# Old states' part of the sampled outputs: C as stationary operand in column strips instead of the state

## What is computed

```python
# G=4 groups, E=8 heads each, P=64 values per head, N=128 state entries
y_diag = jnp.einsum('bcgls,bcgels,bcsgep->bclgep', CB, Lmat, xd)
states = jnp.einsum('bcsgn,bcges,bcsgep->bcgepn', Bm, decay_states, xd)
states = jnp.concatenate([h0.reshape(nb, G, E, P, N)[:, None], states], axis=1)
new_states = jnp.einsum('bgezc,bcgepn->bzgepn', decay_chunk, states)
states_in, final = new_states[:, :-1], new_states[:, -1]
y_off = jnp.einsum('bclgn,bcgepn,bcgel->bclgep', Cm, states_in, jnp.exp(A_cs))
y = (y_diag + y_off).reshape(nb, L, SSD_HEADS, P)
```

## Time and profile before

| | us |
|---|---|
| median of 3 runs | 1894.99 (1893.29 to 1895.34) |
| the profiled execution | 1895.05 |
| its span in the profile | 1892.9 |
| PE busy | 1862.7 (98%) |
| DVE busy | 1111.5 (59%) |
| ACT busy | 647.4 (34%) |
| POOL busy | 137.7 (7%) |

### The profile page before, as it was taken

How to read it: one execution, slowest core, us unless ns; L and a number is a source line. 1 busy time by engine, 2 the same in 40 slices (tenths; PEclk the granted TensorE clock), 3 DMA queues, 4 the chain that set the end, 5 groups by cost and what they waited for, 6 DMA issues and landing times.

```text
span 1892.9 us, 31449 instructions
## 1 busy us (share of the span) xinstructions
PE 1862.7 (98%) x12735; PEld 1817.8 (96%) x12735; DVE 1111.5 (59%) x1368; ACT 647.4 (34%) x842; POOL 137.7 (7%) x257
## 2 busy tenths in 40 slices
PE   8999999999999999999999999999999999999998
PEld 7999999999999999999989989998999999999998
DVE  6443443345777866767777877885855433442444
ACT  5221332123577742334244235233332211221223
POOL 3000000000012121111111101100200000000000
PEclk9999999999999999999999999999999999999999
DMA  5222222222422253354354335335622222222222
GB/s 147 73 71 78 73 72 78 78 67 66 133 69 79 62 160 99 115 153 112 90 151 125 101 95 164 107 106 189 208 70 78 70 74 78 77 67 78 78 64 81
DMA packets 273342, 186.14 MB, mean 98 GB/s; under 512 B 7452, under 2 KB 260580, under 8 KB 273008
## 3 DMA queue, kind: packets, MB, share of 16 engines
q1 hardware_dynamic: 239840, 129.52, 23.8%
q0 software_dynamic: 10624, 36.91, 6.4%
q10 hardware_dynamic: 22800, 18.62, 3.0%
HBM read 162.48 MB, written 22.53 MB: 98 GB/s over the span
## 4 chain that ended last, share of the span: by engine, by line
PE 88%; DVE 6%; ACT 3%; issue 2%; DMA 0%; ACTq 0%; DVEq 0%
PE pu L647 80%; PE pn L899 1%; PE pn L849 1%; DVE w_lo L1403 1%; PE pn L867 1%; PE pn L744 1%; PE pn L871 1%; PE pn L890 1%; PE pu L706 0%; DVE bc L1397 0%; DVE squares L1397 0%; PE pn L838 0%; PE pu L909 0%; PE pn L664 0%; DVE xc L1397 0%
## 5 line engine op out<-in xcount | busy, mean ns | idle before, releaser
L1403 DVE TENSOR_TENSOR w_lo<-w_raw,w_hi 128x1024 fp32r<-128x1024 f32 x240 | 296.5, 1235 | 460.2 <-ACT w_hi L985 458.7
L647 PE MATMUL pu<-act_hi,w_hi 128*128 128x320 f32 x1952 | 456.9, 315 | 6.7 <-DVE xc L1397 2.2
L647 PE MATMUL pu<-act_lo,w_hi 128*128 128x320 f32 x1952 | 447.2, 310 | 1.1 <-DVE act_lo L1446 1.0
L647 PE MATMUL pu<-act_hi,w_lo 128*128 128x320 f32 x1952 | 446.7, 310 | 0.0
L985 ACT ACTIVATE w_hi<-w_raw 128x1024 fp32r<-128x1024 f32 x240 | 253.5, 1056 | 520.8 <-PE pu L647 519.6
L647 PEld LDWEIGHTS pu<-act_hi,w_hi 128*128 128x128 f32 x1952 | 327.3, 189 | 21.3 <-issue 17.1
L647 PEld LDWEIGHTS pu<-act_lo,w_hi 128*128 128x128 f32 x1952 | 328.5, 189 | 2.4 <-DVE act_lo L1446 1.5
L647 PE MATMUL pu<-x_hi,w_hi 128*128 128x320 f32 x1440 | 329.3, 310 | 1.3 <-DVE ff_g L1459 1.3
L647 PEld LDWEIGHTS pu<-act_hi,w_lo 128*128 128x128 f32 x1952 | 328.7, 189 | 0.0
L647 PE MATMUL pu<-x_lo,w_hi 128*128 128x320 f32 x1440 | 328.5, 309 | 0.0
L647 PE MATMUL pu<-x_hi,w_lo 128*128 128x320 f32 x1440 | 328.4, 309 | 0.0
(11 more groups left out here) (318 smaller groups left out, 1924.3 us busy)
## 6 DMA issues: line engine op xcount, KB each, us to landing
w_raw<-in_ffn_w_up_dram SPq DMA_DIRECT2D x87, 512.0 KB, 3.8
w_raw<-in_w_in_dram SPq DMA_DIRECT2D x73, 512.0 KB, 3.9
w_raw<-in_ffn_w_down_dram SPq DMA_DIRECT2D x32, 512.0 KB, 3.8
da_rep<-e_spill POOLq DMA_DIRECT2D x20, 512.0 KB, 4.3
w_raw<-in_w_br_ssd_dram SPq DMA_DIRECT2D x16, 512.0 KB, 3.5
w_raw<-in_ffn_w_down_dram SPq DMA_DIRECT2D x16, 384.0 KB, 3.4
gate_spill<-gbuf ACTq DMA_DIRECT2D x18, 320.0 KB, 2.4
es<-e_spill POOLq DMA_DIRECT2D x40, 128.0 KB, 3.9
```

The costliest lines, as they stand in the source:

```text
L647: ins = pe.matmul(dst[:, h, :], w[:, side, c, :], a[:, k, h * HALF:(h + 1) * HALF], start=(at == 0), stop=(at == n - 1))
L1403: dve.tensor_tensor(w_lo[:, side, :, :], w_raw[:, side, :, :], w_hi[:, side, :, :].bitcast(F32), ALU.subtract).then_inc(s["w_lo_done"], 1)
```

## The change

`from_state` is turned round. Now C is the stationary operand: for one half `qq` (two pairs) the product of all 8 streams is 8 matmuls, each with a 128x32 block of C in one of four 32-column strips of the array and 256 moving columns (both pairs' states of one stream). A strip holds the tokens of two streams, 2j and 2j+1. Since a strip's 32 output partitions are both streams' tokens, C is laid out twice (`c_half`): once with the odd streams' columns zero, once with the even ones', and the two matmuls of a strip are added up in PSUM. The result has tokens by head values, so ACT copies it to `fs_tok` and PE turns it back with two transposes a half (`from_state_rows`) to where `outputs(4)` reads it. `c_half` and `fs_tok` lie where `xd` lies, which is free once `inner(4)` is done; POOL zeroes and fills `c_half` then, behind `b_seq`. The strips' results go to parts of `pn[0]` and `pn[1]` that are free at the time. ACT's `old_copy(1, .)`, which overwrites `h0_t`, now waits for the first half's strips.

```diff
+            with ExitStack() as late:
+                c_half = sb(late, "c_half", [P, 2, P])
+                fs_tok = sb(late, "fs_tok", [P, 2 * NS])
             xd = sb(sc, "xd", [P, HPG, HD])
...
+                pool.wait_ge(s["ssd_p"], g * SP_GRP + SP * (NT - 1) + SP_YD)
+                pool.memset(c_half[:, :, :], 0.0).then_inc(s["c_split"], 1)
+                pool.wait_ge(s["c_split"], 3 * g + 1)
+                for e in range(2):
+                    pool.tensor_copy(sampled(c_half[:, e, :])[:, e::2, :], sampled(xft(g, 5)[:, SEQ:TOK])[:, e::2, :]).then_inc(s["c_split"], 1)
...
-                def from_state(qq, a):
-
-                    q = 2 * qq + a
-                    pe.wait_ge(s["old_cp"], g * 4 + q + 1)
-                    for b in range(DEC_B):
-                        c = SEQ + b * DEC_L
-                        ins = pe.matmul(pn[0][:, 1, q * P + b * DEC_L:q * P + (b + 1) * DEC_L], h0_t[:, a, b, :],
-                                        xft(g, 5)[:, c:c + DEC_L], start=True, stop=True)
+                fs_at = (pn[0][:, 1, 2 * P:4 * P], pn[1][:, 0, 0:2 * P])
+
+                def from_state(qq):
+
+                    pe.wait_ge(s["old_cp"], g * 4 + 2 * qq + 2)
+                    pe.wait_ge(s["c_split"], 3 * g + 3)
+                    for e in range(2):
+                        for j in range(DEC_B // 2):
+                            rows = slice(32 * j, 32 * (j + 1))
+                            ins = pe.matmul(fs_at[qq][rows, :], c_half[:, e, rows], h0_t[:, :, 2 * j + e, :],
+                                            start=(e == 0), stop=(e == 1))
+                    ins.then_inc(s["fs_mm"], 1)
+
+                def from_state_rows(qq):
+
+                    pe.wait_ge(s["fs_cp"], g * 2 + qq + 1)
+                    for a in range(2):
+                        q = 2 * qq + a
+                        ins = pe.transpose(pn[0][:, 1, q * P:(q + 1) * P], fs_tok[:, a * NS:(a + 1) * NS], ident[:, :])
                     return ins
...
-                fill([middle], {0: lambda: old_state(0, 1), 1: lambda: from_state(0, 0), 2: lambda: old_state(1, 0),
-                                4: lambda: from_state(0, 1), 5: lambda: old_state(1, 1)})
+                fill([middle], {0: lambda: old_state(0, 1), 2: lambda: from_state(0), 3: lambda: old_state(1, 0),
+                                5: lambda: old_state(1, 1), 6: lambda: from_state_rows(0)})
                 new_state(1)
-                fill([late], {0: lambda: from_state(1, 0), 2: lambda: from_state(1, 1).then_inc(s["ssd_p"], 1)})
+                fill([late], {0: lambda: from_state(1), 3: lambda: from_state_rows(1).then_inc(s["ssd_p"], 1)})
...
+                    if qq:
+                        act.wait_ge(s["fs_mm"], g * 2 + 1)
...
+                def from_state_copy(qq):
+
+                    act.wait_ge(s["fs_mm"], g * 2 + qq + 1)
+                    src = (pn[0][:, 1, 2 * P:4 * P], pn[1][:, 0, 0:2 * P])[qq]
+                    act.activation(fs_tok[:, :], src, ACT.Copy).then_inc(s["fs_cp"], 1)
```

4 lines of the change are left out of this document (3 added, 1 removed).

## The result

| | before | after |
|---|---|---|
| median | 1894.14 us (4 runs, 1890.18 to 1895.34) | 1875.09 us (4 runs, 1873.41 to 1875.43) |
| profiled execution | 1895.05 us | 1874.83 us |
| its span | 1892.9 us | 1873.1 us |

The ratio is 0.9903 [0.9888, 0.9919] (with its 95% interval; it is taken from all runs and need not be that of the medians): the changed kernel is faster by 19 us. The forecast was 1876.4 us, the range 1873.0 to 1883.5.

What follows compares the result with a forecast made beforehand. PE was taken to bound the kernel, busy 1862.7 of 1892.9 us. The sum 17.0 (halves) - 0.7 (VectorE) - 0.8 (GpSimd) + 3.1 (clock) = 18.6 us, off 1895.05, gave 1876.4 us; range 1873.0 to 1883.5.

Steps and rivals of the forecast that it cites:

- The step that goes: Old states on PE: 8 matmuls with 16 moving columns cost 1.79 us a step, two steps or 3.58 us a half.
- the block that comes: A half's strip matmuls on PE: all four strips at once, 0.86 us streaming plus 0.37 entering and leaving, 1.23 us.
- The transposes: Turning the strips' result back on PE: two transposes a half at 0.11 us each, 0.22 us.
- VectorE's limit: At the late unit PE waits for the accumulator VectorE frees, giving back 0.35 + 3 x 0.1 = 0.7 us.
- GpSimd: The new memset and small copies may slow DVE while PE waits for it: 0.2 us a group, 0.8 in all.
- The fetch: Late unit's spilled gate, ahead of ScalarE's second copy: copy done after 4.3 us, wanted at 4.8; hidden, 0.5 us to spare.
- The clock: Clock falls in the late units of the four groups go away: 3.1 us gained in the sum.
- 1 (two at a time): Strips in program order or two at a time: 2.09 us a block, 1882.6 us in all; chance 0.11.
- 2 (the middle half's gain turns into a wait): VectorE does not move; PE waits 2.1 us more at each group's late-unit accumulator: 1884.3 us; chance 0.05.
- 3 (the clock stretches stay or move): Strips work, but clock falls stay or move to other places: 15.5 us gained, 1879.5 us; chance 0.27.
- 4 (one behind another): Strips share one moving stream, so passes run one behind another: 4.03 us a half against 3.58, 1899.4 us; chance 0.04.
- 5 (the second copy late): Second copy or zeroed C late; PE waits at from_state_rows or from_state(0), some 0.5 us a group: 1878.4 us; chance 0.05.

Runs made afterwards that it cites:

- two_strips: Changed kernel with two 64-column strips of C, four matmuls in each, instead of four 32-column strips: 1879.38 us, ratio 0.9928 to the kernel before.
- strip_major: Changed kernel with the two loops of the strips' matmuls exchanged, so both matmuls of one strip are issued before the next strip's: 1874.39 us, ratio 0.9903.
- one_strip: Changed kernel with all 128 columns of C stationary, all 8 matmuls of a half added up in the same 128 output partitions: 1890.56 us, ratio 0.9993.
- pool_fourfold: Changed kernel with GpSimd zeroing c_half four times instead of once in each group: 1874.66 us, ratio 0.9902.

## Why the prediction was right, point by point

**The step that goes** (1.79 us, 3.58 a half) **and the block that comes** (1.23 us): right. The block is 1.21 us. The working from L849 (0.86 us of streaming and 0.37 of entering and leaving) held for four strips though the trace had two, and `two_strips` confirms it at a second point. The choice against strict program order, argued from L909's 1.13 us, is confirmed by `strip_major`. The transposes cost 0.22 us as worked out from the eight of L890. Passes, transposes and steps come to 2.15 us a half instead of 2.13: 17.2 us against 17.0.

Four strips took 1.00 us of passes, of which 0.86 is what full overlap gives. The Trainium skill's 2.38x for three strips (TensorE: Matmul & The Clock Gate, Part 3, Measured speedup vs the span model) carried over as the prediction did it would have given 1.46 us a block, so here the measurement decides for the sum by the rows. The prediction charged that loss on the streaming alone and put the 0.37 us on top; taken over the whole block, the gain over one strip is 3.46 / 1.21, 2.9 times with four strips. The Trainium skill's rule on the same page (Part 3, The mechanism), that matmuls start and end strictly in program order, doesn't hold for these fp32 passes: strip_major took 1.02 us, where program order would have taken 2.8.

**VectorE's limit**, -0.7 us forecast, -0.24 measured. The mechanism was right: DVE's idle of 1.93 to 2.24 us ahead of the second `decay_states` is gone, and PE waits longer at the late unit of group 0 (0.78 us; the forecast said 0.6 to 1.0, and in the other three groups this sign did not come). The mis-sized term is the 0.1 us for each of the other three groups, where PE waits 0.52 us as before, and 0.11 us in group 0.

**GpSimd**, -0.8 us forecast, 0 measured. The step that failed is the one that took DVE's loss beside `b_seq` (0.85 us for 2 us) as a price per us of any GpSimd work. Memset and copies did not behave like it; the lower bound, 0, was right.

**The fetch**, not in the sum, -0.76 us measured. The text followed the fetch, but only as something that the second copy stands behind. That cover was right for the profile of after: the copy ends at 966.71 in group 1, and PE asks for it 4.8 us into the unit, at 967.05, so 0.34 us were to spare where 0.5 was forecast. What I didn't ask is when the fetch's own data is wanted: 8.7 us after its issue began before (972.99 to 981.69), and with the half's 2.15 us gone, 6.55 us. It took 5.9 us to land before, so this question would still have been answered with "covered, by 0.7 us"; the page of before, with a median of 5.6 us for this fetch, says the same. It took 6.8 us in after. So two things failed: the fetch had no term, and the time that a transfer takes to land was not the same after the change. This cost as much as the GpSimd term had wrongly set aside, so that the two errors cancel. That is luck.

**The clock**, 3.1 us forecast, 3.07 in the profiled pair. The direction is shown (5 of 20 late units against none of 32). The size came out by luck: it is an accident of the profile I read: the average was about one stretch an execution, so about 1.5 us. With one stretch instead of two the gain of the kernel itself is 17.2 - 0.2 - 0.8 + 1.5 = 17.7 us, and the medians of all runs (1893.1 for the 53 of before; 1875.0 for the 12 of after, strip_major and pool_fourfold, which do the same on PE) differ by 18.1 us. The forecast of 18.6 is that close because the median of the first runs of before, 1894.99, lies with the profiled execution in the upper part of the scatter.

**The rivals.** 1 (two at a time) gave its 2.09 us only where two strips were built. 2 (the middle half's gain turns into a wait) had the right place, but 0.24 us of it instead of 8.5. 3 (the clock stretches stay or move) was wrong for the late units; in one of eight profiles with strips a stretch stood elsewhere in the groups. 4 (one behind another) would have been what `one_strip` does: 3.46 us a block, where it was priced at 3.81, since next to nothing is lost in entering and leaving with 128 columns. The time was about that of before instead of slower, since the clock stretches of the late units, which this rival kept, went too, and GpSimd cost nothing. 5 (the second copy late) missed by 0.34 us in group 1 of after, and came true with 0.17 and 0.20 us there in two other profiles of the change's order; the zeroed C was never late.

## What to carry to other kernels

When a product has few moving columns and many stationary operands, exchange the two and put blocks of the small one into column strips: it pays only through the streaming side by side, so work out passes x columns / strips (0.215 us for a pass of 256 columns here) plus 0.35 us for a block, and compare that with the weight loads saved; the exchange alone gave nothing. After a gain on the bounding engine, list every transfer that is issued at a fixed place behind it and subtract the gain from its slack, and leave a margin for landing later: a fetch that landed 2.8 us early was late after a gain of 2.15, since it also took 0.9 us longer. And take a term that comes from low clock in one profile as a sample, not as a property of the kernel, until versions shifted in time show it too.

## What the runs showed of the hardware

- Four 32-column strips of fp32 matmuls run side by side: 16 passes of 256 columns in 1.00 us, where passes through the same columns come 0.215 us apart and one strip takes 3.26. Four passes start within 20 ns. Each strip had its own moving data.
- The order of the passes in the code doesn't matter (1.02 against 1.00 us): a pass that waits for its strip doesn't hold up the others.
- Entering and leaving the tiling cost 0.35 us with four strips and 0.37 with two, once a block.
- GpSimd's memset beside DVE's cut of the weights cost the cut nothing (1.20 us beside, 1.21 alone); beside `b_seq` it took 2.06. GpSimd's copies that started behind the cut took 1.18 us instead of 0.68.
- A fetch of 320 KB issued behind two stores of 512 KB landed 5.9 us after its issue began in the old kernel and 6.8 us in the new one (groups 1 and 3); ahead of them it landed after 4.9 and 4.8 us.
- The same kernel shows a stretch of 3.4 us at half the clock at different places in different executions, also where nothing ahead of it differs, and in some places not at all.
